# A two-layer hybrid attention trunk: scores of the differential branch in three passes of 32 rows, with a reordered opening and tail

## The reference, cut to what matters

```python
def diff_attention(q, k, v, lam):          # q,k [B,T,H,2,32]; v [B,T,H,64]
        s = jnp.einsum('bqhcd,bkhcd->bhcqk', qb, k).astype(jnp.float32) * scale
        p = jax.nn.softmax(jnp.where(causal, s, -jnp.inf), axis=-1)
        pd = (p[:, :, 0] - lam * p[:, :, 1]).astype(v.dtype)
        return jnp.einsum('bhqk,bkhd->bqhd', pd, v)
...
    h = layer_norm(x, ln0_g, ln0_b)
    for l in range(DEPTH):
        h = hybrid_layer(h, mem, ...)      # ends in layer_norm(DN_ALPHA * x + out, ln_g, ln_b)
```

## Time and profile before

| | |
|---|---|
| median of 3 runs | 1427.48 us (1426.43 to 1430.05) |
| the profiled execution's own time | 1427.85 us |
| its span in the trace | 1425.9 us |
| mean granted clock of PE | 0.976 of full speed |
| PE busy | 1343.3 us, 94% |
| DVE, ACT, POOL busy | 717.4, 656.4, 569.6 us |

### The profile page before, as it was taken

The page is one execution under the profiler, slowest core; times in us unless marked ns, Lnnn a source line. Parts: engine busy times, 40 slices in busy tenths (PEclk is TensorE's granted clock), DMA queues, the critical chain, the costliest instruction groups (busy, mean ns, idle before and its releaser), DMA issues. The chain is left out here.

```text
span 1425.9 us, 18920 instructions
## 1 busy us (share of the span) xinstructions
PE 1343.3 (94%) x6872; PEld 1138.0 (80%) x6872; DVE 717.4 (50%) x1713; ACT 656.4 (46%) x1298; POOL 569.6 (40%) x687
## 2 busy tenths in 40 slices
PE   6999999999988899999999999999999789999995
PEld 5877788888877698888888778888888678888884
DVE  5657746543246654323275673763422665543245
ACT  4455335464265555433145542555534564654232
POOL 2443353342542244235445334424345322523453
PEclk9899999999999999999999999999999989999998
DMA  6322242132331133342313213323124201423221
GB/s 247 113 74 59 61 111 74 46 89 60 100 92 33 31 96 86 88 118 76 129 48 103 66 48 97 95 72 83 45 74 111 62 25 49 113 73 93 91 75 59
DMA packets 146842, 116.46 MB, mean 82 GB/s; under 512 B 5440, under 2 KB 131776, under 8 KB 146496
## 3 DMA queue, kind: packets, MB, share of 16 engines
q1 hardware_dynamic: 146608, 114.22, 27.6%
q10 hardware_dynamic: 144, 1.05, 0.2%
HBM read 112.10 MB, written 3.15 MB: 81 GB/s over the span
## 5 line engine op out<-in xcount | busy, mean ns | idle before, releaser
L655 POOL TENSOR_TENSOR weights_rest<-raw_weights,weights_head 128x320 fp32r<-128x320 f32 (+3 forms) x672 | 547.0, 845 | 797.1 <-ACT weights_head L933 797.0
L671 PE MATMUL product<-weights_head,stationary_head 128*128 128x512 f32 (+3 forms) x768 | 292.8, 381 | 3.6 <-POOL weights_rest L655 3.6
L933 ACT ACTIVATE weights_head<-raw_weights 128x1280 fp32r<-128x1280 f32 (+4 forms) x178 | 197.9, 1114 | 207.4 <-PE product L673 161.8
L672 PE MATMUL product<-weights_rest,stationary_head 128*128 128x512 f32 (+3 forms) x768 | 287.2, 374 | 0.0
L673 PE MATMUL product<-weights_head,stationary_rest 128*128 128x512 f32 (+3 forms) x768 | 286.9, 374 | 0.0
L671 PE MATMUL product<-stationary_head,weights_head 128*128 128x512 f32 x640 | 265.4, 415 | 0.0
L673 PE MATMUL product<-stationary_head,weights_rest 128*128 128x512 f32 x640 | 254.3, 397 | 0.0
L672 PE MATMUL product<-stationary_rest,weights_head 128*128 128x512 f32 x640 | 254.0, 397 | 0.0
L1042 ACT ACTIVATE probabilities<-probabilities,negated_maxima 128x256 f32<-128x256 f32 (+3 forms) x160 | 86.6, 541 | 210.6 <-DVE negated_maxima L1321 210.3
L671 PEld LDWEIGHTS product<-weights_head,stationary_head 128*128 128x128 f32 x768 | 146.8, 191 | 25.2 <-POOL weights_rest L655 4.1
L673 PEld LDWEIGHTS product<-weights_head,stationary_rest 128*128 128x128 f32 x768 | 146.7, 191 | 23.8
(11 more groups left out here) (200 smaller groups left out, 1805.0 us busy)
## 6 DMA issues: line engine op xcount, KB each, us to landing
raw_weights<-in_w_in_dram SPq DMA_DIRECT2D x104, 512.0 KB, 3.8
raw_weights<-in_w_in_dram SPq DMA_DIRECT2D x72, 256.0 KB, 3.0
raw_weights<-in_w_branch_dram SPq DMA_DIRECT2D x80, 128.0 KB, 3.9
raw_weights<-in_w_out_dram SPq DMA_DIRECT2D x16, 512.0 KB, 3.6
merged<-in_w_mem_kv_dram SPq DMA_DIRECT2D x4, 1024.0 KB, 8.8
raw_weights<-in_w_in_dram SPq DMA_DIRECT2D x8, 416.0 KB, 3.2
raw_weights<-in_w_in_dram SPq DMA_DIRECT2D x8, 296.0 KB, 4.0
residual<-in_x_dram SPq DMA_DIRECT2D x4, 512.0 KB, 12.4
```

What stands on the lines that cost most here:

```text
L655: ins = nc.gpsimd.tensor_tensor(WL[:, sw, part], RAW[:, sr, part], WH[:, sw, part].bitcast(F32), ALU.subtract)
L671: nc.tensor.matmul(dst, sh, mh, start=start, stop=False)
L672: nc.tensor.matmul(dst, sh, ml, start=False, stop=False)
L933: return nc.scalar.activation(dst, src, ACT.Copy, scale=scale)
```

## The change

**C's maps.** `ev` runs for j = 0 and j = 2 only, each for two heads with their four maps: ACT copies all 128 rows of q and of k once, DVE subtracts twice, 128 rows each. The operands of all four heads stay resident in eight slots of TL (no wait for older scores). A map stays in its 32 rows, and a score is three passes (head by head, head by rest, rest by head) of 32 rows each, at `tile_position` (32 m, 0). `diff_steps()` has 61 entries for 62, so all scores fall on other groups.

**Opening.** The constants are loaded in two parts, the second (mask, rotary tables) after the first three weight units; `w_mem_kv` comes in four quarters between the tiles of x; POOL's bias add is four instructions of 256 columns; the first weight split comes behind the first `xj`, the other two behind `xj` of tile 1, in both layers.

**Tail.** For tile 3 `l1` is now (x - mean) * gain on DVE, `l2` is times 1/deviation plus bias in two halves, with a store behind each; ACT's `normalize` of that tile is gone.

```diff
 def diff_steps():
-    out = [[("qt", "C", 0)], [("ev", "C", 0, 0)], [("ev", "C", 0, 1)], [], []]
+    out = [[("qt", "C", 0)], [("ev", "C", 0)], [], []]
...
-        if i == 4:
-            third.append(("qt", "C", 1))
-        j, m = divmod(i + 3, 4)
-        if j < NH and m < 2 and i < UNITS:
-            third.append(("ev", "C", j, m))
+        if i in (2, 3):
+            third.append(("qt", "C", 1) if i == 2 else ("ev", "C", 2))
...
-    start = [("split",) + w for w in WEIGHTS[:3]]
-    start += [("mkv", 0), ("xj", 0, 0), ("xj", 0, 1), ("mkv", 1), ("xj", 1, 0), ("xj", 1, 1)]
+    splits = [("split",) + w for w in WEIGHTS[:3]]
+    start = [("mkv", 0), ("xj", 0, 0), ("xj", 0, 1), splits[0], ("mkv", 1), ("xj", 1, 0), ("xj", 1, 1), splits[1], splits[2]]
...
             for t in range(2):
                 sp.dma_start(MEM_IN[:, t], mem[0, t * P:(t + 1) * P, :]).then_inc(mem_in[t].sem, mem_in[t].step(("first", "m"), 16))
-            sp.dma_start(CN[:, P:], consts[:, P:]).then_inc(first_in.sem, first_in.step(("first", "c"), 16))
+            new_layer(mk_in, 0)
             load_x(0)
             load_mk(0, 0)
...
             load_x(1)
...
+            load_mk(0, 1)
             load_x(2)
+            load_mk(0, 2)
             load_x(3)
-            load_mk(0, 1)
+            load_mk(0, 3)
...
-                nc.gpsimd.tensor_tensor(X[:, t, :], X[:, t, :], b, ALU.add).then_inc(normed.sem, normed.step(key))
+                for i in range(4):
+                    part = slice(i * 256, (i + 1) * 256)
+                    ins = nc.gpsimd.tensor_tensor(X[:, t, part], X[:, t, part], b[:, part], ALU.add)
+                ins.then_inc(normed.sem, normed.step(key))
...
-                            at = 4 * (j % 2) + 2 * (u % 2)
-                            passes = [(TL[0:96, at, q], TL[0:96, at + 1, 0:w])]
+                            row = 32 * (2 * (j % 2) + u % 2)
+                            qh, ql, kh, kl = (TL[row:row + 32, 4 * (j // 2) + i] for i in range(4))
+                            passes = [(qh[:, q], kh[:, 0:w]), (qh[:, q], kl[:, 0:w]), (ql[:, q], kh[:, 0:w])]
...
-                            last = nc.tensor.matmul(S[:, 0:w], lhs, rhs, start=i == 0, stop=i == len(passes) - 1)
+                            last = nc.tensor.matmul(S[:, 0:w], lhs, rhs, start=i == 0, stop=i == len(passes) - 1,
+                                                    tile_position=(row if b == "C" else 0, 0))
...
+                            copy(TL[:, 4 * e, :], qs[:]).then_inc(moved.sem, moved.step(("evq", b, j)))
                             act.wait_ge(t_done.sem, t_done.at(L, ("k", b, e)))
-                            copy(TL[64:96, slot, :], qs[r, :])
-                            copy(TL[0:32, slot, :], qs[r, :]).then_inc(moved.sem, moved.step(("evq", b, j, m)))
-                            copy(TL[32:64, slot + 1, :], ks[r, :])
-                            copy(TL[0:32, slot + 1, :], ks[r, :]).then_inc(moved.sem, moved.step(("evk", b, j, m)))
+                            copy(TL[:, 4 * e + 2, :], ks[:]).then_inc(moved.sem, moved.step(("evk", b, j)))
...
+                            go(nc.vector.scalar_tensor_tensor(out=X[:, t, :], in0=X[:, t, :], scalar=BN[:, 4 * t:4 * t + 1],
+                                                              in1=LN_IN[:, 0:D], op0=ALU.subtract, op1=ALU.mult))
...
+                            for j in range(2):
+                                half = slice(j * 512, (j + 1) * 512)
+                                nc.vector.scalar_tensor_tensor(out=X[:, t, half], in0=X[:, t, half], scalar=BN[:, 4 * t + 2:4 * t + 3],
+                                                               in1=LN_IN[:, D + j * 512:D + (j + 1) * 512], op0=ALU.mult,
+                                                               op1=ALU.add).then_inc(gained.sem, note(gained, ("last", j)))
```

More of the change, by code:

```diff
@@ L397, in build @@
         O = ctx.enter_context(nc.psum_tensor("context", [P, 512], F32))
-        mk_in = [tally(f"memory_weights_loaded{i}") for i in range(2)]
+        mk_in = [tally(f"memory_weights_loaded{i}") for i in range(4)]
         raw = [tally(f"raw_loaded{i}") for i in range(NRAW)]
@@ L555, in _ @@
                 for i, item in enumerate(LOADS):
+                    if L == 0 and i == NRAW:
+                        sp.dma_start(CN[:, C_MASK:], consts[:, C_MASK:]).then_inc(first_in.sem, first_in.step(("first", "c"), 16))
                     s = i % NRAW
@@ L616, in _ @@
                     sp.wait_ge(rest.sem, rest.at(L, ("m", KD - 1)))
[L617 to L623, removed]
-                sp.dma_start(out[0, t * P:(t + 1) * P, :], X[:, t, :]).then_inc(stored.sem, stored.step(("first", t), 16))
-            sp.wait_ge(stored.sem, stored.at(0, ("first", NT - 1)))
+                    for i in range(4):
+                        load_mk(L + 1, i)
+            for t in range(NT - 1):
+                sp.wait_ge(normed.sem, normed.at(DEPTH - 1, ("t", t)))
+                sp.dma_start(out[0, t * P:(t + 1) * P, :], X[:, t, :]).then_inc(stored.sem, stored.step(("first", t), 16))
+            for j in range(2):
+                half = slice(j * 512, (j + 1) * 512)
+                sp.wait_ge(gained.sem, gained.at(DEPTH - 1, ("last", j)))
+                sp.dma_start(out[0, (NT - 1) * P:NT * P, half], X[:, NT - 1, half]).then_inc(stored.sem, stored.step(("first", NT - 1 + j), 16))
+            sp.wait_ge(stored.sem, stored.at(0, ("first", NT)))
         @block.gpsimd
@@ L783, in _ @@
                         elif t == NT - 1:
-                            pe.wait_ge(gained.sem, gained.at(L - 1, ("last",)))
+                            pe.wait_ge(gained.sem, gained.at(L - 1, ("last", j)))
                         else:
@@ L1006, in _ @@
                         e = j if b == "D" else j // 2
-                        if j >= 2 and b != "E":
+                        if j >= 2 and b not in "EC":
                             act.wait_ge(s_done.sem, s_done.at(L, ("S", b, 8 * (j - 2) + 7 if b == "C" else 4 * (j - 2) + 3)))
@@ L1187, in _ @@
                                     ALU.add).then_inc(gained.sem, note(gained, ("first", "last")))
+            dve.wait_ge(first_in.sem, first_in.at(0, ("first", "c")))
             for L in range(DEPTH):
@@ L1198, in _ @@
                     elif kind == "l1":
[L1199 to L1206 removed]
+                        t = step[1]
+                        if t < NT - 1:
+                            scale(L, t, ("ln", t), ("t", t))
+                        else:
+                            dve.wait_ge(summed.sem, summed.at(L, ("ln", t)))
+                            go(nc.vector.scalar_tensor_tensor(out=X[:, t, :], in0=X[:, t, :], scalar=BN[:, 4 * t:4 * t + 1],
+                                                              in1=LN_IN[:, 0:D], op0=ALU.subtract, op1=ALU.mult))
+                    elif kind == "l2":
+                        t = step[1]
+                        if t < NT - 1:
+                            gain(L, t, ("t", t), LN_IN[:, 0:D])
+                        else:
+                            dve.wait_ge(rooted.sem, rooted.at(L, ("ln", t)))
+                            chain(nc.vector.reciprocal(BN[:, 4 * t + 2:4 * t + 3], DEV[:, t:t + 1]))
+                            for j in range(2):
+                                half = slice(j * 512, (j + 1) * 512)
+                                nc.vector.scalar_tensor_tensor(out=X[:, t, half], in0=X[:, t, half], scalar=BN[:, 4 * t + 2:4 * t + 3],
+                                                               in1=LN_IN[:, D + j * 512:D + (j + 1) * 512], op0=ALU.mult,
+                                                               op1=ALU.add).then_inc(gained.sem, note(gained, ("last", j)))
                     elif kind == "mj":
```

54 lines of the change are left out of this document (22 added, 32 removed).

## The result

| | before | changed |
|---|---|---|
| median of the runs, us | 1428.76 (1426.43 to 1431.71) | 1452.08 (1446.81 to 1452.89) |
| profiled execution, us | 1427.85 | 1451.45 |
| its span, us | 1425.9 | 1449.8 |

The changed kernel is slower: ratio 1.016, interval 1.014 to 1.018. Forecast were 1422.0 us and a gain. The time is above the range too (1406 to 1441), and on the side of rival B.

The account below looks back on a forecast made before the run. PE, busy 94% of the span, was taken to bound the kernel, waiting mostly for DVE; 20.6 + 3.8 - 18.5 - 5.6 - 5.8 + 2 - 2 = -5.5 gave 1422.0 us, range 1406 to 1441.

Parts of the forecast that it names:

- rival B: Around C's 64 scores: each switch drains PE, 0.16 us, 20.5 in place of 3.8, so 1438.7 us; chance 0.22.
- Switching: C's scores: 128 switches between 128-row and 32-row passes at 0.03 us each, +3.8 us, from 0 to +44.
- the threshold (0.07): Price per switch in us from which C's switching would use up the whole forecast gain.
- The rest of C: Branch C without switching: passes +20.6, stalls -18.5, clock -5.6 us.
- The passes: C's 64 scores: three passes in place of one, 0.32 us more in the mean, +20.6 us on PE.
- PE's idle time in C: Stalls in C: 15.9 us a layer falls to about 6.7, -18.5 us, from -10 to -26.
- The clock: PE's granted clock in C: 0.91 rises to 0.95 or more, -5.6 us, from 0 to -12.
- Both signs of being wrong: Spacing around scores grows over 0.1 us a switch; PE's waits for `negated_maxima` stay above 20 us in the span.
- Opening: Start of the kernel: PE's first product near 34 us in place of 39.63, -5.8 us, from -2 to -8.
- Boundary: Between the layers: the second group waits for the later second weight split, +2 us, from 0 to +4.
- Tail: End of the kernel: DVE ends about 3 us earlier, the last landing a little later, -2 us, from -1 to -3.5.

Follow-up runs that it names:

- e1: The changed kernel with C's three passes laid over all 128 rows, so no change of tile size; 1429.06 us, 1.0005 of the kernel before.
- e3: The changed kernel with one pass a score in C instead of three, two changes of tile size a score kept; 1442.48 us, 1.0105.
- e6: The kernel before with only the changed opening, boundary and tail, second weight split put back ahead of the memory's second half; 1423.72 us, 0.9973.
- e7: e6 with the last layer's norm wholly on DVE for all four tiles, no ACT or POOL in the tail; 1419.85 us, 0.9951.

## Why the prediction was wrong

*Switching: +3.8 forecast, +21 to +23 measured.* This is the term that failed, and with it the sign. Between the kernel with 128 changes of tile size and the one with none are 1452.08 - 1429.06 = 23.0 us, and 21.3 at C's place alone: 0.17 to 0.18 a change. PE itself pays more, since it idles 3.2 us more for DVE without the changes. In the rows at the full clock, from the product ahead of a score to the second behind it, the changed kernel takes 0.34, 0.40, 0.40 and 0.41 us more than e1 at the four widths, 0.19 a change. I named the two ends of the price rightly (0 and 0.35 us) and then took 0.03, "near the lower end", because the nearest row was a product behind a short score. That row has no change of tile size in it; it priced something else. Rival B had the mechanism, the place and the threshold (0.07), and nearly the price (0.16). It had 0.22, and a term whose upper end is 44 us, with no row of its own kind, ought to have had more. The Trainium skill, TensorEngine Tiling (Array Packing), Tiling Modes, says that a change of tiling mode, and not just of tile, drains TensorE. These runs agree: the weight load is no longer pulled ahead, and the cost is near the overlap of two passes (0.16) that a drain would give up. That it is this overlap, and nothing else of the same size, is a reading of the rows and was not tested.

*The rest of C: -3.5 forecast (20.6 - 18.5 - 5.6), -0.4 measured* (e1 against the kernel before, at C's place). The passes cost what was forecast: e3 and the changed kernel have the same changes and one pass against three, and their rows differ by 0.23, 0.24, 0.35 and 0.46 us at the four widths, 20.4 us for 64 scores. (The forecast's own four differences give 20.8, not 20.6.) PE's idle time in C fell from 15.9 to 7.7 us a layer, 16.4 in both where 18.5 were forecast; its waits for DVE were forecast at 6.65 us and came to 3.02, 2.35, 0.45 and two smaller ones of 0.53 and 1.28 further on, 7.6 in all, largely at the places named, with norm work at t = 3 as what is late next. The clock rose from 0.91 to 0.95, as forecast. Both signs of being wrong that the prediction named appeared: the spacing around a score grew by over 0.1 us a change, and the waits for `negated_maxima` stayed above 20 us, at 21.4. Of these 15.3 are in C; the threshold left little room for the 6 outside it.

*Opening: -5.8 forecast, -4.2 measured* at the first product, which starts at 35.38 us (forecast "near 34", before 39.63). DVE's one-element row fell from 2.33 to 0.71 us, as said.

*Boundary: +2 forecast, +4.2 measured.* The wait is the one forecast (2.46 for 2.1), in the forecast place; I put "some loss of clock" to nothing in the number, and 5 us at 1.2 GHz are 2.5. e6 shows it: with the split put back the 4.2 us are gone from this place.

*Tail: -2 forecast, +1.8 measured.* DVE does end 3 us earlier against PE's last pass. I had followed DVE and not POOL: I costed the quarters by what DVE loses to them, never by what they lose to DVE, 4.04 us a tile in the mean in place of 2.35, and so the store of tile 2 became the last thing. e7 shows that POOL was the limit: without it the tail is 4.3 us shorter. Whole adds under the new form of tile 3 were not tried.

So of the 29.4 us between the forecast -5.5 and the +23.9 of the span, switching is 17.5, the rest of C 3.1, the tail 3.8, the boundary 2.2 and the opening 1.6; 3.0 are the stall in E, which the forecast did not have and whose cause is open, less the 1.7 of the stretch ahead of C. Without the first the time would have stood inside the range.

## What to carry to other kernels

Passes that use another part of the array are not priced by their columns alone: count the changes of tile size (here 0.18 us each, on the engine that bounds the kernel) before counting copies saved elsewhere. When an operand costs too many copies, look first whether an engine stands in its queue waiting for another one's copies; moving the dependent half one step back gave 13.8 us with nothing removed. And a term without a row of its own kind should take its price from the middle of its bounds, and lend its upper end to the chances.

## What the runs showed of the hardware

- A change between 128-row and 32-row tiles costs PE 0.17 to 0.20 us, as the mean of the two directions (23.0 us for 128 changes; 0.39 and 0.41 us for two in the rows of 512 columns). The weight load behind it starts with its own pass, 0.2 us later than between equal tiles.
- It is the change that costs, not the 32 rows: a pair of changes adds 0.39 us with one 32-row pass between them (e3) and 0.41 with three.
- DVE and POOL slow each other in both directions when both work on two tensors in SBUF. POOL's add of a tile takes 2.35 us whole, beside DVE's product too, which then pays (3.32 us in place of 1.2). In quarters both pay: a quarter takes 0.72 us with no DVE product beside it and 1.70 to 1.77 beside one, and the DVE product 1.74. DVE's statistics keep their 0.69 us beside POOL's quarters.
